# Expert results added into x3 in DRAM by an accumulating scatter, instead of written to two tables and added at the end

## The reference, cut to what matters

```python
x = x + (gt_a * out)                                  # called x3 in the kernel
h2 = modulate(rmsnorm(x, norm2_g), sh_m, sc_m)
x = x + gt_m * hier_moe(h2, w_router_group, w_router_expert, w_expert_in, w_expert_out)
return rmsnorm(x, final_norm_g)

def hier_moe(h, w_rg, w_re, w_e_in, w_e_out):
    pg = softmax(t @ w_rg); gp, gi = top_k(pg, 1)     # one of 4 groups of 8 experts
    le = (t @ w_re).reshape(-1, 4, 8)[gi]             # the group's 8 experts
    ew, ei = top_k(softmax(le), 2)                    # two experts of that group
    weights = gp * ew / sum(ew);  eid = gi * 8 + ei
    for wi, wo, ge in experts:                        # 32 experts, ge: weight per token, 0 if not chosen
        a, u = split(t @ wi, 2)                       # wi 1024 x 512
        acc += ((silu(a) * u) @ wo) * ge[:, None]     # wo 256 x 1024
```

## Time and profile before

| | us |
|---|---|
| median of 3 runs | 1640.46 (1639.87 to 1645.15) |
| the profiled execution: its own time | 1644.79 |
| the profiled execution: span from the first to the last instruction | 1642.9 |
| PE, DVE, ACT, POOL busy in the span | 1461.7, 703.2, 378.8, 316.9 |
| mean granted clock of PE | 0.963 |
| data moved | 232.59 MB |

### The profile page before, as it was taken

The page is one execution under the profiler, slowest core; times in us unless marked ns, Lnnn a source line. Parts: engine busy times, 40 slices in busy tenths (PEclk is TensorE's granted clock), DMA queues, the critical chain, the costliest instruction groups (busy, mean ns, idle before and its releaser), DMA issues. The chain is left out here.

```text
span 1642.9 us, 22231 instructions
## 1 busy us (share of the span) xinstructions
PE 1461.7 (89%) x8638; PEld 985.6 (60%) x8638; DVE 703.2 (43%) x1226; ACT 378.8 (23%) x799; POOL 316.9 (19%) x269
## 2 busy tenths in 40 slices
PE   5999999999999979989999999999989977888782
PEld 4864446884544457778888778673757764332220
DVE  5252344123369957775332144310354445332324
ACT  3224445104333333322100122301231010000001
POOL 3420021520007255534630000000000001111110
PEclk9999999999999979999999999999998978999996
DMA  5237110303112124414332040422033257999995
GB/s 186 81 121 237 52 54 24 103 26 128 52 52 77 59 71 130 131 52 168 127 129 77 0 129 26 73 72 67 22 123 111 95 204 310 425 421 426 422 378 219
DMA packets 119545, 232.59 MB, mean 142 GB/s; under 512 B 13329, under 2 KB 103023, under 8 KB 110483
## 3 DMA queue, kind: packets, MB, share of 16 engines
q1 hardware_dynamic: 114115, 220.54, 37.5%
q0 software_dynamic: 5184, 8.55, 1.4%
q10 hardware_dynamic: 144, 2.10, 0.3%
HBM read 223.65 MB, written 17.84 MB: 147 GB/s over the span
## 5 line engine op out<-in xcount | busy, mean ns | idle before, releaser
L962 PE MATMUL psv<-arena 128*128 128x256 f32 x1008 | 221.5, 379 | 2.1 <-issue 2.1
L962 PEld LDWEIGHTS psv<-arena 128*128 128x128 f32 x1008 | 191.1, 190 | 30.2 <-issue 4.4
L924 PE MATMUL psv<-arena,wslot 128*128 128x512 f32 x384 | 170.8, 598 | 1.8 <-DVEq L2214 1.8
L1634 ACT ACTIVATE arena<-pss 128x512 f32<-128x512 f32 (+1 forms) x157 | 84.8, 540 | 330.2 <-PE pss L924 276.3
L1549 PE MATMUL pss<-arena 128*64 128x512 f32 x432 | 118.0, 618 | 14.5 <-DMA arena<-w_expert_in 11.9
L924 PEld LDWEIGHTS psv<-arena,wslot 128*128 128x128 f32 x384 | 71.1, 190 | 85.5 <-issue 83.0
L924 PE MATMUL pss<-arena 128*128 128x256 f32 (+1 forms) x384 | 113.6, 453 | 5.8 <-ACTq L152 3.1
L2230 DVE TENSOR_TENSOR arena<-arena,psv 128x512 f32<-128x512 f32 x66 | 45.4, 687 | 163.5 <-PE psv L962 161.3
L2445 DVE SCALAR_TENSOR_TENSOR arena<-psv,ccols,arena 128x510 f32<-128x510 f32 (+1 forms) x96 | 71.9, 749 | 59.9 <-ACT arena L1801 56.8
L924 PEld LDWEIGHTS pss<-arena 128*128 128x128 f32 x384 | 71.7, 190 | 41.1 <-issue 28.4
L924 PE MATMUL psv<-wslot,arena 128*128 128x256 f32 x416 | 93.1, 385 | 3.0 <-DMA wslot<-w_in 2.6
(11 more groups left out here) (346 smaller groups left out, 2014.5 us busy)
## 6 DMA issues: line engine op xcount, KB each, us to landing
arena<-w_expert_in SPq DMA_DIRECT2D x27, 2048.0 KB, 26.8
wslot<-w_in SPq DMA_DIRECT2D x32, 1024.0 KB, 5.5
arena<-w_expert_out SPq DMA_DIRECT2D x32, 1024.0 KB, 27.3
wslot<-w_ada SPq DMA_DIRECT2D x18, 1024.0 KB, 5.4
arena<-w_in SPq DMA_DIRECT2D x10, 1024.0 KB, 6.8
wslot<-w_expert_in SPq DMA_DIRECT2D x5, 2048.0 KB, 21.5
arena<-w_ada SPq DMA_DIRECT2D x6, 1024.0 KB, 9.0
arena<-x SPq DMA_DIRECT2D x8, 512.0 KB, 7.9
```

Source lines behind the costliest of these rows:

```text
L924: m = mm(o, l, r, start=(n == 0), stop=(n == len(pairs) - 1))
L962: m = mm(o[:, j * HALF_T:(j + 1) * HALF_T], l[:, c, j * P:(j + 1) * P], r[:, c, :], start=new and j == 0 and c == 0, stop=j == 1 and c == ...
L1634: L.did(A(dst, src, func, **kw), s[sig] if sig else None, [s["free_s"]])
```

## The change

Five things change together.

- The scatter adds (`compute_op=ALU.add`) into `x3_dram`, which has a spare row 512 now, instead of writing to `y_dram`, which is gone. Its index list is the gather's, `index`.
- The weight of a row must now be in the row before it is scattered. DVE puts the weights into tables like the tokens (`wpick`, `wgt_at`), PE makes a second product of 32 matmuls for them, DVE copies it to `w_slot`, and `hidden` multiplies by the weight of the row as well (one instruction as before, with one operand more).
- Pair n is now experts n and n+16. Two experts of one pair then lie in different groups, so a token stands at most once in a scatter.
- `list_tokens` shrinks from five instructions to one.
- At the end SP waits for the last scatters, loads only x3 (four tiles, no longer ahead of them), and DVE's eight multiply-adds are gone. ACT waits for each tile's load, then DVE for ACT.

```diff
@@ -88,8 +88,8 @@
-    c[:, C_EPS + 3] = np.where(i < P - 1, NOWHERE, 2 * SEQ)
-    c[:, C_TOK:C_TOK + 2 * NT] = p + P * (np.arange(2 * NT) // 2) + SEQ * (np.arange(2 * NT) % 2) - NOWHERE
+    c[:, C_EPS + 3] = np.where(i < P - 1, NOWHERE, SEQ)
+    c[:, C_TOK:C_TOK + 2 * NT] = p + P * (np.arange(2 * NT) // 2) - NOWHERE
@@ -423,7 +423,7 @@
-        y_index = at(top[0], ROUNDS * NP).bitcast(U32)
+        w_slot = at(top[0], ROUNDS * NP)
@@ -432,14 +432,14 @@
+        wgt_at = at(top[0], NT, 2, ROUNDS, NE)
...
-        row_f = at(top[0], ROUNDS * NP)
-        row_k = at(top[0], ROUNDS * NP)
+        wpick = at(top[0], NT, 2, NE)
@@ -449,8 +449,7 @@
-        y_dram = scratch("y_dram", 2 * SEQ + 1, DM)
-        x3_dram = scratch("x3_dram", SEQ, DM)
+        x3_dram = scratch("x3_dram", SEQ + 1, DM)
@@ -551,8 +550,8 @@
-        win_src = a["w_expert_in_2"][0].rearrange("(i x) (p c) n -> i x p c n", x=2, p=P)
-        wout_src = a["w_expert_out_2"][0].rearrange("(i x) (p c) n -> i x p c n", x=2, p=P)
+        win_src = a["w_expert_in_2"][0].rearrange("(x i) (p c) n -> i x p c n", x=2, p=P)
+        wout_src = a["w_expert_out_2"][0].rearrange("(x i) (p c) n -> i x p c n", x=2, p=P)
@@ -743,8 +742,8 @@
             def save(t):
...
-                load(xn_dram[t * P:(t + 1) * P, :], x3n[:, t, :], "xn_saved")
-                load(x3_dram[t * P:(t + 1) * P, :], x3[:, t, :], "x3_saved")
+                load(xn_dram[t * P:(t + 1) * P, :], x3n[:, t, :], "rows_saved")
+                load(x3_dram[t * P:(t + 1) * P, :], x3[:, t, :], "rows_saved")
@@ -827,20 +826,20 @@
-            load(xn_dram[SEQ:, :].rearrange("o (p n) -> (o p) n", p=KC), zero[0:KC, :], "xn_saved")
+            for rows_ in (xn_dram, x3_dram):
+                load(rows_[SEQ:, :].rearrange("o (p n) -> (o p) n", p=KC), zero[0:KC, :], "rows_saved")
...
             sp.wait_ge(s["lg_ready"], 1)
-            sp.wait_ge(s["xn_saved"], 16 * (NT + 1))
-            sp.wait_ge(s["x3_saved"], 16 * NT)
+            sp.wait_ge(s["rows_saved"], 2 * 16 * (NT + 1))
...
-            sp.wait_ge(s["index_ready"], 2)
+            sp.wait_ge(s["index_ready"], 3)
@@ -870,16 +869,11 @@
-            sp.wait_ge(s["win_used"], rounds * NP)
-            for t in range(NT):
-                load(x3[:, t, :], x3_dram[t * P:(t + 1) * P, :], "x3_saved")
...
-                sp.wait_ge(s[f"st_y{k}"], rounds * (NP // 2 * 16) + 16)
-            for t in range(NT):
-                for k in range(2):
-                    sp.dma_start(ygat[:, k, t, :], y_dram[k * SEQ + t * P:k * SEQ + (t + 1) * P, :])\
-                        .then_inc(s["ygat_ready", t], 16)
+                sp.wait_ge(s[f"st_y{k}"], rounds * (HALF * 16) + 16)
+            for t in range(NT):
+                sp.dma_start(x3[:, t, :], x3_dram[t * P:(t + 1) * P, :]).then_inc(s["x3_back", t], 16)
@@ -1515,7 +1509,7 @@
-                    slots = rtok[:, t, k, :].rearrange("p (i x) -> p i x", x=2)
+                    slots = rtok[:, t, k, :].rearrange("p (x i) -> p i x", x=2)
@@ -1528,15 +1522,16 @@
-            o = bank("v")
-            for t in range(NT):
-                L.need(s["table_ready"])
-                for k in range(2):
-                    slots = tok_at[:, t, k, :, :].rearrange("p r (i x) -> p (r i) x", x=2)
-                    for x in range(2):
-                        m = mm(o[x * CAP:(x + 1) * CAP, 0:ROUNDS * NP], rplaced[:, 2 * t + k, :], slots[:, :, x],
-                               start=(t == 0 and k == 0), stop=(t == NT - 1 and k == 1))
-            m.then_inc(s["full_v"], 1)
+            for table in (tok_at, wgt_at):
+                o = bank("v")
+                for t in range(NT):
+                    L.need(s["table_ready"])
+                    for k in range(2):
+                        for x in range(2):
+                            m = mm(o[x * CAP:(x + 1) * CAP, 0:ROUNDS * NP], rplaced[:, 2 * t + k, :],
+                                   table[:, t, k, :, x * NP:(x + 1) * NP], start=(t == 0 and k == 0),
+                                   stop=(t == NT - 1 and k == 1))
+                m.then_inc(s["full_v"], 1)
@@ -1993,7 +1988,7 @@
-                act.wait_ge(s["x3_ready"], NT + t + 1)
+                act.wait_ge(s["x3_back", t], 16)
@@ -2148,7 +2143,7 @@
-            pool.wait_ge(s["xn_saved"], 16 * (NT + 1))
+            pool.wait_ge(s["rows_saved"], 2 * 16 * (NT + 1))
...
                 nc.gpsimd.indirect_dma_start(
@@ -2157,8 +2152,8 @@
             def scatter(k, rows_):
                 nc.gpsimd.indirect_dma_start(
-                    y_dram, bass.IndirectOffsetOnAxis(ycol[:, k:k + 1], 0), rows_, None,
-                    bounds_check=2 * SEQ, oob_is_err=False).then_inc(s[f"st_y{k}"], 16)
+                    x3_dram, bass.IndirectOffsetOnAxis(ycol[:, k:k + 1], 0), rows_, None,
+                    bounds_check=SEQ, oob_is_err=False, compute_op=ALU.add).then_inc(s[f"st_y{k}"], 16)
@@ -2183,7 +2178,7 @@
             def result(i, k):
...
-                list_rows(ycol, k, y_index[:, bass.ds(i * 2 + k, 1)])
+                list_rows(ycol, k, index[:, bass.ds(i * 2 + k, 1)])
@@ -2840,14 +2835,8 @@
             def list_tokens(c0, c1):
...
-                L.did(V.tensor_scalar(row_f[:, c0:c1], b[:, c0:c1], float(NOWHERE), spare, ALU.add, ALU.min), s["free_v"])
-                L.did(V.tensor_scalar(row_k[:, c0:c1], row_f[:, c0:c1], float(SEQ), float(-SEQ), ALU.is_ge, ALU.mult))
-                add(row_k[:, c0:c1], row_k[:, c0:c1], row_f[:, c0:c1])
-                if c0:
-                    L.did(V.tensor_copy(y_index[:, c0:c1], row_f[:, c0:c1]))
-                L.did(V.tensor_copy(index[:, c0:c1], row_k[:, c0:c1]), s["index_ready"])
-                if not c0:
-                    L.did(V.tensor_copy(y_index[:, c0:c1], row_f[:, c0:c1]))
+                L.did(V.tensor_scalar(index[:, c0:c1], b[:, c0:c1], float(NOWHERE), spare, ALU.add, ALU.min),
+                      s["index_ready"], [s["free_v"]])
@@ -2858,22 +2847,28 @@
-            L.did(V.tensor_scalar(index[:, ROUNDS * NP:], spare.broadcast_to([P, 4]), float(-SEQ), None, ALU.add))
+            L.did(V.tensor_copy(index[:, ROUNDS * NP:], spare.broadcast_to([P, 4])))
...
+            mul(wpick, pick, ewt.unsqueeze(3).broadcast_to([P, NT, 2, NE]))
+            for t in range(NT):
+                mul(wgt_at[:, t], wpick[:, t].unsqueeze(2).broadcast_to([P, 2, ROUNDS, NE]),
+                    rround[:, 2 * t:2 * t + 2, :].unsqueeze(3).broadcast_to([P, 2, ROUNDS, NE]), s["table_ready"])
+            b = full()
+            L.did(V.tensor_copy(w_slot, b[:, 0:ROUNDS * NP]), s["free_v"], [s["index_ready"]])
...
-            def hidden(k, job):
+            def hidden(k, job, w):
...
-                L.did(V.tensor_tensor(hid[:, k, :], pss[:, (s0 + job) % 4, DE:2 * DE], sil[:, k, :], ALU.mult),
-                      s["hid_ready"], [s["free_s"], s["sil_used"]])
+                L.did(V.scalar_tensor_tensor(hid[:, k, :], pss[:, (s0 + job) % 4, DE:2 * DE], w, sil[:, k, :],
+                                             ALU.mult, ALU.mult), s["hid_ready"], [s["free_s"], s["sil_used"]])
@@ -2903,11 +2898,11 @@
-                hidden(0, 0)
+                hidden(0, 0, w_slot[:, bass.ds(r * NP, 1)])
...
-                        hidden(1 - k, 2 * n + 1)
+                        hidden(1 - k, 2 * n + 1, w_slot[:, bass.ds(r * NP + (n + 1), 1)])
@@ -2915,20 +2910,12 @@
-            dve.wait_ge(s["x3_saved"], 2 * 16 * NT)
...
-            for t in range(NT + 1):
-                if t < NT:
-                    dve.wait_ge(s["ygat_ready", t], 32)
-                    for k in range(2):
-                        L.did(V.scalar_tensor_tensor(x3[:, t, :], ygat[:, k, t, :], ewt[:, t, k:k + 1], x3[:, t, :],
-                                                     ALU.mult, ALU.add), s["x3_ready"] if k else None)
-                if t:
-                    L.need(s["rs_out"])
-                    r = ss[:, t - 1:t]
-                    L.did(V.reciprocal(r, r))
-                    L.did(V.scalar_tensor_tensor(x3[:, t - 1, :], x3[:, t - 1, :], r, rowf, ALU.mult, ALU.mult),
-                          s["out_ready"])
+            for t in range(NT):
+                L.need(s["rs_out"])
+                r = ss[:, t:t + 1]
+                L.did(V.reciprocal(r, r))
+                L.did(V.scalar_tensor_tensor(x3[:, t, :], x3[:, t, :], r, rowf, ALU.mult, ALU.mult), s["out_ready"])
```

More of the change, by code:

```diff
@@ L466, in build @@
             sprev_ready sc_ready o2_ready sq2_ready rt2_ready cat_ready x3_ready h3_ready lg_ready
-            lexp_ready ld_out win_used wout_used ld_gs yb_ready hidT_ready sil_ready hid_ready out_ready picked_ready icol_ready xn_saved x3_saved gla_used first_ready
+            lexp_ready ld_out win_used wout_used ld_gs yb_ready hidT_ready sil_ready hid_ready out_ready picked_ready icol_ready rows_saved gla_used first_ready
             table_ready index_ready xg_k0 xg_k1 xe_ready st_y0 st_y1
@@ L476, in build @@
```

(2 more changed lines are left out.)

## The result

| | before | after |
|---|---|---|
| median of 7 runs each, us | 1640.23 (1636.78 to 1645.15) | 1648.29 (1643.5 to 1655.3) |
| the profiled execution, its own time | 1644.79 | 1648.57 |
| its span | 1642.9 | 1646.8 |
| mean granted clock of PE | 0.963 | 0.960 |

The ratio is 1.0051, with a 95% interval of 1.003 to 1.0072: the kernel became slower by 8.1 us by the medians, 4.9 to 11.8 by the interval. The forecast was 1639.7, no change; the time lies within the range of 1631 to 1658, on the side that was called slower.

What follows compares the result with a forecast made beforehand. It took the full DMA engines to bound the expert loop and DVE's chain the end. The terms -9.5 + 0.6 - 0.4 + 0 + 8.5 = -0.8 us gave 1639.7 from the median; range 1631 to 1658.

Steps and rivals of the forecast that it cites:

- What bounds: Expert loop: DMA engines full, so each further byte before the last weights ends it later; at the end, DVE's chain.
- In the loop, DMA: Expert loop: 13 accumulating scatters each read 0.262 MB once more, in competition with the weights, +8.5 us; bounds 0 and 17.
- In the loop, the rest: Expert loop, engines' own work: small additions covered by PE's products, 0 us; 3 if the cover were gone.
- `hidden` and the index list: Expert loop: one instruction with one operand more, and an index column that is the same copy, 0 us.
- The routing: Ahead of the loop: shorter lists bring the gather 0.6 earlier, the weights' table fits PE's wait; -0.4 us, bounds 0 and +0.7.
- The end from SP's first load on: Kernel's end: DVE's eight multiply-adds and half the loaded bytes go, -9.5 us; first x3 tile there after 3.8.
- The last scatter: After the loop: it also reads x3 rows, 0.262 MB at 423 GB/s, +0.6 us; bounds nothing and another 2.92.
- 1.5 late: Last index column: if the previous scatter's landing took twice 2.92, it would exceed the 4.31 us available and come 1.5 late.
- The free read: Rival, in the loop: the addition's read costs nothing or nearly so, -9.3 us in all, 1631.2; chance 0.18.
- Three passes a row: Rival, in the loop: an added row costs an engine three passes, +17 in place of +8.5, 1648.2; chance 0.12.
- The chain of landings: Rival, in the loop: scatters waiting for each other's landings bound it if added rows take two turns, +25, 1656; chance 0.28.
- the point: In the loop: the scatter landing time, 13.8 us, from which waits between scatters decide a pair's length of 14.8.

Runs made afterwards that it cites:

- no addition: After with plain scatters that overwrite x3 in DRAM, so the sums are left out; 1634.21 us, 0.9954 of before.
- last two plain: After with the scatters of the last two pairs plain, overwriting x3, while the others still add; 1644.59 us, 1.0014 of before.
- every second addition: After with additions only in the scatters of even pairs up to 12; odd pairs and the last two plain; 1636.44 us, 0.9976 of before.
- DVE's end split: Before with DVE's last product for tiles 0 and 1 at the end replaced by products on ACT and POOL; 1642.56 us, 1.0007 of before.
- extra read: After with plain scatters, and ahead of each an indirect gather of half rows (2 KB) into an unused place; 1640.37 us, 1.0 of before.

## Why the prediction was right or wrong

**What bounds: right.** The DMA engines are full in the loop and the weights pay for every other transfer. The waits of PE from 1376 to 1610 show it, of after first, then of no addition (total us, times, longest):

```profile
PE pss L1544 <- DMA arena<-w_expert_in: 19.8, 8, 4.9
```
```profile
PE pss L1544 <- DMA arena<-w_expert_in: 15.2, 6, 3.8
```

I had named about 24 for after; it is 19.8. The +10.0 at pair 15 is more than the growth of these waits, because PE's clock was low for longer. The stretch from the first product of pair 0 to that of pair 15, before and then after:

```profile
1378.83:1594.77 215.94, 181.58 (x845) 67.93 (x845) 67.23 (x103) 12.39 (x30) 35.28 (x59) 0.98 0.98 408
```
```profile
1377.24:1603.17 225.93, 188.00 (x844) 69.40 (x845) 68.17 (x103) 12.42 (x30) 43.60 (x60) 0.95 0.98 392
```

PE did the same work in 188.0 instead of 181.6 us of busy time, at a granted clock of 0.95 instead of 0.98, and was idle for 37.9 instead of 34.4: 6.4 and 3.6 make the 10.0. After has first products of 8.8 to 10.1 us instead of 7.09 behind most of its waits for weights. Since the DMA engines' share is 1.01 from 1390 to 1592 in both kernels, they and not PE set the pace there; the slower products fill time in which PE would have waited.

**In the loop, DMA: +8.5, measured +10.0 against before and +10.3 against no addition. Mechanism right, size a little low.** The price can be read from single packets of POOL's queue with a whole row of 4 KB, over the full trace (number of packets on either side of 243 ns, and the median of each side where there are additions):

```text
                       under      over
before                  2054        30
after                   1008      1076      159 and 327 ns
no addition             2045        39
last two plain          1145       939      159 and 327 ns
every second addition   1597       487      159 and 327 ns
```

A row that is added takes its engine 327 ns instead of 159, in one packet as before. 30 to 39 packets are over 243 ns without any addition, so about 1040 of the 1076 are added rows: two for each token and a spare one in each of the 16 scatters of results, 65 a scatter. 65 x 168 ns / 16 engines = 0.68 us by this, where the sum had 0.65; 13 scatters were right. The queues from the first product of pair 0 to the landing of the last `w_expert_in`, after first (225.72 us), then no addition (215.43 us):

```profile
q1 hardware_dynamic: 7403, 81.20, 85.2%
q0 software_dynamic: 4122, 7.22, 12.5%
```
```profile
q1 hardware_dynamic: 7311, 80.55, 88.7%
q0 software_dynamic: 4084, 7.22, 9.1%
```

POOL's queue took 28.2 instead of 19.6 us of all engines, 8.6 for the same 7.22 MB: that is the forecast's term. SP's took 1.2 us more, since 0.65 MB more of weights were moved by then, and 0.5 of the 10.3 is in neither. These 1.7 us are what the sum had left out here; why more of the weights go ahead of the last `w_expert_in` isn't known.

The Trainium skill, "Collectives: The Full Stack", section "The bandwidth ceiling", has a reducing transfer read with two descriptors on one ring, at half the rate. By that rule the trace agrees: 327 ns is 2.06 times 159.

**In the loop, the rest: 0, measured +1.7.** The first product of pair 15 began after an idle 2.38 us of PE and ran at a granted clock of 0.56 from 1604 to 1606 in the stretches above, about the lower of its two levels (1.2 GHz of 2.4), and took 8.78 instead of 7.09 us. It was 8.5 to 8.8 in the four kernels where PE had waited 2.37 us or longer ahead of it, and 7.09 in the four where it had waited 1.79 or less. But within the loop waits of 3.47 and 3.52 us in before were followed by products of 7.09, and one of 1.96 in after by a product of 8.79, so the length of the wait alone doesn't decide it, and I don't know what does. It is seen, not explained. It isn't the addition's either: the kernel without addition has it, and so has the one with DVE's end split, which has nothing of the change. I had costed the engines by their instructions and no later wait by its clock.

**`hidden` and the index list: 0, right.** `hidden` takes 0.48 us, an instruction of DVE in the timeline at L2870, and no part of the loop grew without the addition.

**The routing: -0.4, measured +0.8. Wrong in sign.** Against before it is +0.8 to +1.0 in four of the five kernels that have the second table (+0.3 in the fifth, the extra read), and -0.4 and 0 in the two that have not. Rows of its timeline in after show the steps that failed:

```profile
1361.14 0.71 POOL L2160 COPY arena<-arena 128x1 uint32<-128x1 uint32 x1 [26.19 <-DVE arena L2838]
1362.85 1.52 POOL L2149 DMA_INDIRECT arena<-xn_dram,arena  x1 [0.99 <-POOLq L2162]
1364.26 2.46 PE L1531 MATMUL psv<-arena 128*64 128x128 f32 x32
...
1367.83 0.33 DVE L2838 TENSOR_SCALAR arena<-psv,const 128x112 uint32<-128x112 f32 x1 [0.53 <-PE psv L1531]
...
1369.62 2.75 PE L1531 MATMUL psv<-arena 128*64 128x128 f32 x32 [2.89 <-DVE arena L2222]
1372.48 0.29 DVE L2861 COPY arena<-psv 128x128 f32<-128x128 f32 x1 [0.83 <-PE psv L1531]
1372.89 2.05 PE L1538 MATMUL psv<-const,arena 128*128 128x128 f32 x16 [0.53 <-DVE arena L2861]
```

The shorter list did give POOL its index earlier, but POOL's copy took 0.71 instead of 0.18 us, and the gather was issued 29.70 us after the memset instead of 29.78: nothing gained. PE's matmuls of the first table began at +31.1 (us after the memset) in both kernels (1364.26 here, 1366.61 in the earlier trace rows), so DVE's second list ended at +35.0 and not at the +34.5 of the forecast. And the second table's matmuls, which I had let end in the shadow of the gather at +38.4, ended at +39.2. Behind them stands DVE's copy into `w_slot`, for which PE's transposes wait and which I hadn't put between the two: they began at +39.7, where they had begun at +39.1 before. The landing of the gather is no longer what PE waits for there. The upper bound of +0.7 was nearly right, the middle was not.

**The end from SP's first load on: -9.5, measured -10.1. Right.** ACT is idle only ahead of the first tile, and the four tiles follow each other by 1.52 us in DVE's products, as worked out. The first tile came 3.23 us after its issue instead of 3.8, which is the 0.6.

**The last scatter: +0.6, measured +2.8 and +1.2. This is the step that failed most.** I took 0.262 MB at the mean rate of sixteen full engines. Nothing competes at the end of the kernel, and still the scatter took longer than that: its packets ran from first start to last end for 1.04 us before (67 rows), 1.27 without the addition and 3.20 with it (71 rows). 71 rows over 16 engines are 4.4 each on average. The trace doesn't number the engines, but 1.27 us are eight packets of 159 ns one behind the other, so I estimate eight rows on the fullest. 8 x 327 ns is 2.6 us; the rest is at the start, where each of the first sixteen rows took 0.45 to 1.27 us instead of 0.33, for a reason that no run here shows. On top of that POOL's own instruction is longer. The rows of the tile x_dram, after first, then no addition (ns: minimum, median, maximum):

```profile
L2154 POOL DMA_INDIRECT x_dram<-arena x16: 1572/1606/1627, 1400.2 to 1625.8; - x16
```
```profile
L2154 POOL DMA_INDIRECT x_dram<-arena x16: 982/1023/1035, 1402.6 to 1616.7; - x16
```

1.61 instead of 1.02 us. Together that is 2.8 us of landing, 0.2 of it by the pairing, and near the upper bound of 2.92 that the prediction gave and did not take. The same 5.4 us of the scatter before it no longer fit into the 4.31 that were there, so the last index column came 1.2 us late; the prediction had this as the case "1.5 late", and kept it out of the sum and out of the chances. The pair of them is the 3.7 us of after over last two plain (5.67 - 3.14 = 2.5 of landing and 1.2 of waiting).

**The rivals.** The free read falls with the 10.4 us of the loop. Three passes a row falls with 327 ns, twice 159. The chain of landings falls too, though one of its signs came: POOL's index column waited for landings for 9.2 us in seven waits from 1390 to 1602, where it had been 5.6 in five.

```profile
POOL arena L2160 <- DMA x_dram<-arena: 9.2, 7, 1.8
```

The other signs are against it: POOL's queue still has 5184 packets, the landing of a scatter is 13.3 us in the median and the point was 13.8, and seven additions cost 7/13. Where PE waits for weights, the scatters leave 17 us apart (1551.85, 1568.89, 1585.85, 1602.90) and none of the last four waits for a landing. The Trainium skill, "DMA: Bandwidth & Descriptors", section "SWDGE vs HWDGE vs iDMA", gives a packet as preferably at most 4096 B, from which the rival made two turns of an added row; the trace has one packet of twice the time.

**The sum.** Three terms missed in one direction, the loop by 3.1, the end by 2.7 and the routing by 1.2: 7.0 us, which turned -0.8 into +6.2. Of the 3.1 in the loop, 1.7 is the clock at pair 15 and the rest is weights and what no row tells; of the end, +3.4 is the last two scatters and -0.6 the first tile. The loop's DMA term and the 9.5 came out near, so what turned the sum is what I had priced at the mean rate (the last scatters) or at nothing (the wait for the scatter before, the clock, the copy ahead of the transposes). The 2.92 was the row of a scatter at the quiet end of this kernel, and I took 0.6 beside it. And "slower" was given only to rivals, and none of it to a sum of small misses.

## What to carry to other kernels

An addition in DRAM is paid in the DMA engines at two passes a row, and the profile's bytes don't show it; compare the share of the queue. Where these engines are the bound it is charged in full against whatever else they load, so it pays only if the work it spares stands on the path and is longer: here 9.9 us of DVE's end against 10.4 in the loop and 3.7 at the end. Price a transfer in the busy loop by all engines' mean rate, but one that the chain waits for alone by at least its fullest engine and by the issuing instruction; here even that was 0.6 us short.

## What the runs showed of the hardware that I had not expected

- An accumulating row of 4 KB is one packet of 327 ns, a plain one a packet of 159 ns, and the second read stands neither in the queue's MB nor in the memory's (8.55 and 219.46 MB with and without the addition). The memory's line is a weak witness: with the extra read it grew by 4.46 MB, while POOL's queue moved 2.26 MB more.
- GpSimd's instruction for such a scatter takes 1.61 us, for a plain one 1.02.
- The rows of a scatter are spread unevenly over the engines: an estimated 8 on the fullest (1.27 us / 159 ns) where the mean is 4.4.
- The first sixteen rows of a lone accumulating scatter took 0.45 to 1.27 us each, with no other packet beside them; most of the later ones 0.33.
- PE's clock fell to its lower level behind waits from 1.96 us on, but not behind others of up to 3.52.
- GpSimd's product of 128x1024 took 3.42 and 3.11 us beside DVE's multiply-adds, and a pair of those 6.16 instead of 2.61. Elsewhere in the same kernel (L2086, 12 times) the same form takes 2.35 in the mean.
- The time ahead of the routing varies by 5.2 us between profiled executions (the memset at 1330.36 to 1335.51), more than half of the whole effect. Two spans should be laid over each other at a common instruction before they are compared.
